# Weight slots shifted by 16 and 48 bytes a slot, two other orders of a block's three products, and two tiles in runs of 256 columns

## The reference

```python
def swiglu_ffn(x, g, w_gate, w_up, w_down):
    h = rms_norm_2(x, g)
    return (jax.nn.silu(h @ w_gate) * (h @ w_up)) @ w_down      # 1024 -> 2816 -> 1024
...
u = h @ w_in                                                   # and w_out, ple_w_gate, w_proj_a, w_proj_b
```

## Time and profile before

| What | Value |
|---|---|
| Median of 2 runs | 1812.36 us (1812.22 to 1812.49) |
| Span of the profiled execution | 1811.8 us (core 0, mean granted clock 0.996) |
| PE busy | 1780.6 us, 98% |
| PEld busy | 1410.9 us, 78% |
| ACT, DVE, POOL busy | 63%, 50%, 17% |
| HBM read | 162.45 MB, 93 GB/s over the span |

### The profile page before, as it was taken

The page is one execution under the profiler, slowest core; times in us unless marked ns, Lnnn a source line. Parts: engine busy times, 40 slices in busy tenths (PEclk is TensorE's granted clock), DMA queues, the critical chain, the costliest instruction groups (busy, mean ns, idle before and its releaser), DMA issues.

```text
span 1811.8 us, 24236 instructions
## 1 busy us (share of the span) xinstructions
PE 1780.6 (98%) x8915; PEld 1410.9 (78%) x8915; DVE 900.7 (50%) x1588; ACT 1133.6 (63%) x1548; POOL 314.5 (17%) x409
## 2 busy tenths in 40 slices
PE   6999999999999999999999999999999999999999
PEld 4777678777777888888888876767777888888887
DVE  5999658757658573222211165696754432222100
ACT  5777768666667676566644475666675566666433
POOL 1222011322322111111111111001111111111111
PEclk9999999999999999999999999999999999999999
DMA  8898698766665687888889976445656888888897
GB/s 239 187 214 198 160 226 196 184 148 139 151 154 136 161 202 189 192 197 185 198 207 226 231 177 156 116 116 128 151 128 170 202 195 198 192 192 192 202 217 189
DMA packets 94039, 328.05 MB, mean 181 GB/s; under 512 B 12416, under 2 KB 12544, under 8 KB 93184
## 3 DMA queue, kind: packets, MB, share of 16 engines
q0 software_dynamic: 47440, 158.36, 47.7%
q1 hardware_dynamic: 43920, 157.57, 26.8%
q10 hardware_dynamic: 2592, 10.94, 1.7%
HBM read 162.45 MB, written 6.29 MB: 93 GB/s over the span
## 4 chain that ended last, share of the span: by engine, by line
PE 84%; DVE 11%; ACT 3%; issue 1%; DMA 1%; ACTq 0%; DVEq 0%
PE ps L1784 70%; PE ps L1801 3%; DVE cv_acc L1330 3%; DVE tmp L1330 3%; PE ps L1859 2%; PE ps L2054 1%; PE ps L2066 1%; DMA w_lo<-w_raw 1%; PE ps L2312 1%; PE ps L2273 1%; PE ps L2095 1%; PE ps L2357 1%; PE ps L2370 1%; PE ps L2022 1%; PE ps L1820 1%
## 5 line engine op out<-in xcount | busy, mean ns | idle before, releaser
L1784 PE MATMUL ps<-H_hi,w_hi 128*128 128x512 f32 x1256 | 502.4, 400 | 4.5 <-DMA w_lo<-w_raw 4.5
L1784 PE MATMUL ps<-H_hi,w_lo 128*128 128x512 f32 x1256 | 489.5, 390 | 0.0
L1784 PE MATMUL ps<-H_lo,w_hi 128*128 128x512 f32 x1256 | 489.5, 390 | 0.0
L490 POOL DMA_DIRECT2D w_lo<-w_raw x289 | 249.3, 863 | 1364.8 <-ACT w_lo L569 1328.7
L555 ACT ACTIVATE w_hi<-w_raw 128x1024 fp32r<-128x1024 f32 x292 | 306.8, 1051 | 116.7 <-PE ps L1784 111.7
L569 ACT ACTIVATE w_lo<-w_raw 128x1024 fp32r<-128x1024 f32 x292 | 305.1, 1045 | 0.0
L1784 PEld LDWEIGHTS ps<-H_hi,w_hi 128*128 128x128 f32 x1256 | 236.0, 188 | 63.5 <-issue 12.8
L1784 PEld LDWEIGHTS ps<-H_lo,w_hi 128*128 128x128 f32 x1256 | 236.2, 188 | 54.1 <-issue 6.5
L1784 PEld LDWEIGHTS ps<-H_hi,w_lo 128*128 128x128 f32 x1256 | 236.0, 188 | 49.8
L1183 DVE SCALAR_TENSOR_TENSOR X<-ps,X 128x512 f32<-128x512 f32 (+1 forms) x36 | 27.0, 751 | 238.8 <-PE ps L1784 231.2
L1784 PE MATMUL ps<-mid_hi,w_hi 128*128 128x512 f32 x352 | 136.9, 389 | 0.0
(11 more groups left out here) (375 smaller groups left out, 2712.4 us busy)
## 6 DMA issues: line engine op xcount, KB each, us to landing
w_raw<-weights SPq DMA_DIRECT2D x292, 512.0 KB, 4.7
w_lo<-w_raw POOLq DMA_DIRECT2D x289, 512.0 KB, 5.4
cv_yl<-cv_a POOLq DMA_DIRECT2D x8, 256.0 KB, 3.3
pl_P<-spill ACTq DMA_DIRECT2D x1, 2048.0 KB, 9.5
spill<-X ACTq DMA_DIRECT2D x8, 256.0 KB, 5.2
X<-spill ACTq DMA_DIRECT2D x2, 1024.0 KB, 5.8
out<-X SPq DMA_DIRECT2D x8, 256.0 KB, 4.5
at_C<-cv_Y POOLq DMA_DIRECT2D x7, 256.0 KB, 8.4
```

The lines of the kernel that those rows point to most:

```text
L490: pool.dma_start(w_lo[:, u, :], w_raw[:, u, :], accum_op=ALU.add).then_inc(lo_landed[u], 16)
L1784: mm = pe.matmul(ps[:, bank, :], w, x, start=first and n == 0 and q == 0, stop=last and n == len(blocks) - 1 and q == 2, skip_group_check= ...
```

## The change

Four edits, all in what PE reads or in what order.

1. `w_hi` gets rows of 1024 + 4 float32 and `w_lo` rows of 1024 + 12, of which 1024 are used. Slot s of w_hi therefore begins 16 s bytes past a multiple of 64 (0, 16, 32, 48), and slot s of w_lo 48 s bytes past one (0, 48, 32, 16). The two tensors become 64 and 192 bytes longer in each partition, so w_lo begins 64 bytes and all that is allocated behind it (the parameters, the constants, G, N, mid, m, the convolution's and the attention's buffers) 256 bytes later. ACT, the adding DMA and PE's weight loads use the new places; w_raw, X and H stay.
2. In the loop of stage 7 the products of a block stand in the order (0, 2, 1).
3. In the loop of stage 13 they stand in the order (1, 0, 2).
4. In stage 12, of the six tiles that `single` makes (u = 2 to 7), u = 3 and u = 7 have each matmul cut in two of 256 columns, and u = 2 and u = 6 a pattern of two runs of 256 columns in one matmul.

```diff
+HI_SHIFT, LO_SHIFT = 4, 12
...
-        w_hi = sb("w_hi", [P, RING, D], F32R)
-        w_lo = sb("w_lo", [P, RING, D])
+        w_hi = sb("w_hi", [P, RING, D + HI_SHIFT], F32R)[:, :, 0:D]
+        w_lo = sb("w_lo", [P, RING, D + LO_SHIFT])[:, :, 0:D]
...
-                        for q, (w, x) in enumerate(((wh, x_hi), (wh, x_lo), (wl, x_hi))):
-                            mm = pe.matmul(ps[:, bank, :], w, x, start=first and n == 0 and q == 0,
-                                           stop=last and n == len(blocks) - 1 and q == 2,
-                                           skip_group_check=between is not None)
+                        products = ((wh, x_hi), (wh, x_lo), (wl, x_hi))
+                        for q, (w, x) in enumerate(products[o] for o in order):
+                            begun, ends = first and n == 0 and q == 0, last and n == len(blocks) - 1 and q == 2
+                            if halves == 2:
+                                for h in range(2):
+                                    half = slice(S // 2 * h, S // 2 * (h + 1))
+                                    mm = pe.matmul(ps[:, bank, half], w, x[:, half], start=begun and h == 0, stop=ends and h == 1,
+                                                   skip_group_check=True)
+                                continue
+                            if halves == 1:
+                                mm = pe.matmul(ps[:, bank, :].rearrange("p (a b) -> p a b", a=2), w,
+                                               x.rearrange("p (a b) -> p a b", a=2), start=begun, stop=ends)
+                                continue
+                            mm = pe.matmul(ps[:, bank, :], w, x, start=begun, stop=ends, skip_group_check=between is not None)
...
-            up()
+            up((0, 2, 1))
...
-                single(m_hi, m_lo, None, READ0[12] - 1 if u < 4 else 0)
+                single(m_hi, m_lo, None, READ0[12] - 1 if u < 4 else 0, halves=(0, 0, 1, 2)[u % 4])
...
-            up()
+            up((1, 0, 2))
```

More of the change, by code:

```diff
@@ L1766, in _, with tile @@
             k.up(x_summed)
-            def tile(groups, arriving=None, room=None, between=None):
+            def tile(groups, arriving=None, room=None, between=None, order=(0, 1, 2), halves=0):
                 s = k.n.get("tile", 0) % RING
@@ L1842, in blocks, with single, pair @@
                 return [(first + b, hi[:, at + b, :], lo[:, at + b, :]) for b in range(n)]
-            def single(hi, lo, arriving=None, least=0, between=None):
+            def single(hi, lo, arriving=None, least=0, between=None, halves=0):
                 pe.wait_ge(read_out, max(least, k.at(read_out, -3)))
-                tile([(bank_of(k.n["tile"]), True, True, blocks(hi, lo))], arriving, between=between)
+                tile([(bank_of(k.n["tile"]), True, True, blocks(hi, lo))], arriving, between=between, halves=halves)
                 k.up(read_out)
-            def pair(hi, lo, arriving=None):
+            def pair(hi, lo, arriving=None, order=(0, 1, 2)):
                 pe.wait_ge(read_out, k.at(read_out, -1))
                 for n in range(2):
-                    tile([(bank_of(k.n["tile"]), True, True, blocks(hi, lo))], None if n else arriving)
+                    tile([(bank_of(k.n["tile"]), True, True, blocks(hi, lo))], None if n else arriving, order=order)
                 k.up(read_out)
@@ L1892, in down, with up @@
                     k.up(read_out)
-            def up():
+            def up(order):
                 for u in range(2):
@@ L1903, in up @@
                     for u in range(2):
-                        pair(H_hi, H_lo)
+                        pair(H_hi, H_lo, order=order)
                 k.up(split_lo, FF)
```

## The result

The changed kernel takes 1840.64 us in the median (1838.78 to 1842.5, 2 runs) against 1812.36 us. The ratio is 1.0157, with a 95% interval of 1.0128 to 1.0187: 28 us slower, less than the 2% line. The profiled execution has a span of 1836.8 us against 1811.8, so 25.0 us are to be found in the two traces.

The account below looks back on a forecast made before the run. The prediction took PE's matmul stream, 0.2267 us from start to start, as the bound. Profiled 1811.8 + 0 (slots) + 0 (orders) + 3.3 (cut tiles) = 1815.1 us, plus 0.6 to the median: 1816 us; range 1800 to 1852.

Parts of the forecast that it names:

- within two per cent: Whole kernel: a time of 1776 to 1849 us, about what a measurement can tell from no change; chance 0.75.
- a worse steady distance: Rival, feed-forward stream: matmuls with moved weights stay at 0.2309 to 0.2344 us, 1838 to 1856 us in all; chance 0.18.
- The bound: Whole kernel: PE, busy 98% of the span, bounds it with a plain matmul stream at 0.2267 us start to start.
- Part 1, the slots: Moved slots 1 to 3, 5130 matmuls: places off 64 bytes cost zero, between -68 and +40 us.
- The upper term: Moved slots 1 to 3: each matmul lengthens as with shifted streamed operands, 5130 x 0.0077 = +40 us.
- The step from span to median: Whole kernel: the runs' median stands 0.6 us above the profiled span, taking 1815.1 to 1816 us.
- The buffers behind by 256 bytes: G, N, mid and m move by 256 bytes and stay multiples of 64: zero, between the same ends.
- The orders: Loops of stages 7 and 13, 960 reordered matmuls each: zero, between +15 and -26 us.
- The cut tiles: Two stage 12 tiles with 48 matmuls of 256 columns: 7.1 us each, +3.3 us for both.
- A kick at each slot: Rival, head of each tile: eleven matmuls to settle, 285 tiles x 0.046 = +13 us, 1829 us; chance 0.14.
- A better distance: Rival, matmul stream: the 0.0133 us excess shrinks, 1782 us if half goes, 1747 if all; chance 0.12.
- Slower through the DMA: Rival, adding DMA to w_lo's new places: packets half as long again slow down and up loops, about 1920 us; chance 0.08.

Follow-up runs that it names:

- e1_orders_cuts: Kernel before with the new orders of stages 7 and 13 and the cut tiles of stage 12, every buffer at its old place: 1811.9 us, ratio 1.0007.
- the five scans: Kernel before with w_hi and w_lo slots both shifted alike, in steps of 4, 16, 32 or 64 bytes: 1830.77 to 1841.13 us, one run each.
- e11_scan4: Kernel before with rows of D + 1, slots of w_hi and w_lo both 0, 4, 8, 12 bytes past a multiple of 512: 1830.77 us.
- e2_slots: Kernel before with the change's slot shifts, but w_lo beginning at a multiple of 512; old orders, no cut tiles: 1831.97 us, ratio 1.0113.
- e10_lo_alone: Kernel before with only w_lo's slots shifted, to 64, 112, 160, 208 bytes; w_hi at multiples of 512, old orders, no cut tiles: 1840.87 us, ratio 1.0159.

## Why the prediction was right or wrong

The range held 1840.64, and "within two per cent" was the likeliest class, but the range held by a rival's share in it and not by the forecast's reasoning: the time came by **a worse steady distance**, which had a chance of 0.18 and gave 1838 to 1856 us. The forecast itself, 1816 us, was 25 us short. The prediction took two per cent for about what a measurement can tell; the interval of the result is 0.3% to either side, so the 28 us are clear of noise.

- **The bound.** Right. PE's stream was the place to look, and the long pieces of the chain divided by their matmuls showed the loss at once: 0.2321 for 0.2267.
- **Part 1, the slots. This step failed.** It took zero for the slots' places, and they came to about +28 us (1836.8 us against the 1808.4 of e1_orders_cuts, which differs from the change in the places alone). The weight load of L2248 was the wrong measure: it is the length of the load that stayed (188 ns for w_hi, 190 for w_lo after the change), while the distance between matmuls grew. So a load whose recorded end lies well before its matmul is due (190 of 232 ns) still went with a longer distance. The shifted taps of the earlier trace rows were the nearer rows: they changed the relation of the two reads, as the slots do, and every distance there was longer. The upper term, 5130 x 0.0077 = +40 us, came from them; it counted slots 1 to 3 alone, while slot 0 was hit as well, by w_lo's 64 bytes.
- **What hid part of it.** 0.0054 us on 6840 matmuls would be 37 us, and 28 came. In the convolution stage, 600 matmuls of the ring, nothing came: from its first such matmul to that of the next stage are 160.8 us in e1_orders_cuts and in the changed kernel. The chain of the kernel before ran through DVE's taps there (L1330, some 15.7 us for a channel), and after the change it runs through PE's matmuls; PE had waited, and the longer stream filled the waiting. The other 6 us are missing where other work stands between the tiles: the 960 matmuls of stage 4 lost 3.2 us and not 5.2. There tiles took 5.46 to 5.49 us in the chain already before; whether a disturbance that was there before covers part of the new loss was not tested.
- **The step from span to median.** The sum took the median for 0.6 us over the span. An execution's own time stands 2.0 us over its span (1838.78 and 1836.8), and the profiled execution of before was one with the two stretches of low clock; the 0.6 is of two executions. It changes the forecast by less than 2 us.
- **The buffers behind by 256 bytes.** Right at zero: w_lo and all behind it 256 bytes later gives 0.9998.
- **The orders.** Right at zero: 359.07 and 353.66 us again with both new orders.
- **The cut tiles.** +3.3 us forecast, +0.6 measured. The line from 128 to 512 columns put 256 at 0.148 us; it is 0.1198. The price is columns at 2.4 GHz plus 0.013 us at both widths. The 128-column instructions of the earlier trace rows are of another kind, float32 transposes (L2085), and don't lie on that line.
- **A kick at each slot.** Wrong as the main cause. The first matmuls of a tile do differ, but slot 1's tile of 5.60 us is 24 x 0.2333: nearly all is steady.
- **A better distance.** No place in the five scans gave one.
- **Slower through the DMA.** Refuted: landing 5.4 us as before, the adding queue's share 47.3% (was 47.7%).

The Trainium skill's account of separate read ports ("TensorE: Matmul & The Clock Gate", Step-by-step: what each phase is for), by which a load takes nothing from the running matmul, does not hold here as a rule of cost: moving w_lo alone made the kernel 1.59% slower and its stream 2.4% (0.2322 us for 0.2267). What in the reads collides was not seen; the runs show which places are slow, not why; the ports themselves no run shows.

## What to carry to other kernels

Before calling a shift of a stationary operand free, measure the distance from start to start, not the length of the weight load. In a dense float32r stream keep weights and streamed operand at the same place modulo 256 bytes; a row pad of one float32 a slot cost about 1% here (e11_scan4, 1830.77 us in one run), and pads of 4 and 12 cost 1.1% (e2_slots). A ring with a different place in each slot is a cheap way to scan such places in one run, if the streamed operand's place is held.

## What the hardware showed that was not expected

- The distance of two 128 x 512 float32r matmuls with their own loads goes by the weights' start less the streamed operand's, modulo 256 as far as tried: 0.2267 us at 0, 16 and 256 bytes, 0.2333 at 32, 48, 64, 224, 288 and 320, 0.234 at 352, between these at 4, 8, 12, 128, 192, 208 and 240. This is with w_hi and w_lo at the same place.
- 4 bytes (0.232 us) are worse than 16 (0.2267), and 64 bytes are among the worst, so alignment to 64 alone says nothing.
- One misplaced load in three (w_lo alone) can cost as much as three: 0.2311 us in slot 3 of e10_lo_alone and of the change, where w_hi lies 48 bytes off as well. At 64 bytes it costs two thirds of it, 0.0044 of 0.0066 us. How loads affect their neighbours stays open, as does what the steady rhythms come from.
- A matmul costs its columns at 2.4 GHz and 0.013 us more, at 512 and at 256 columns alike. Whether that part can be had back was not found.
